# Joined changes to a five-layer kernel: order of a step in the second attention, square sums, the last projection's sides, Newton

## The chip, the core and the metric

One core of a Trainium2 chip runs the kernel. The metric is device time in microseconds of that core, median of several executions. TensorE multiplies matrices, VectorE and GpSimd do elementwise work, ScalarE activations and copies, and SP issues DMA transfers. In the profile they are PE, DVE, POOL, ACT and SP; PEld is TensorE's weight load.

## What is computed

x has 512 tokens of 1024 numbers, in float32. Four mixers come first (a conformer convolution, a forgetting attention, a short convolution, the conformer again), then one block with two attentions side by side and a feed-forward, then a last norm:

```python
def second_block(x, ...):
    h = rmsnorm(x, norm_mix)
    proj = h @ w_in                       # queries, keys, values of both attentions, gates g_br
    o_a = dsa_mixer(...)                  # 8 heads, one shared key/value, 256 best keys of 512
    o_b = nsa_mixer(...)                  # 8 heads: compressed, selected and window branch
    gate_a, gate_b = jnp.split(g_br, 2, axis=-1)
    mix = sigmoid(gate_a) * (o_a @ w_branch_a) + sigmoid(gate_b) * (o_b @ w_branch_b)
    x = x + mix @ w_out
    h = rmsnorm(x, norm_mlp)
    x = x + jnp.square(jax.nn.relu(h @ w_mlp_in)) @ w_mlp_out
    return rmsnorm(x, norm_final)
```

## The kernel before

x is kept as X, features on partitions: eight tiles of 128 features by 512 tokens. Every large product is made of float32r products of high and low parts, three for each pair of tiles (HH by WH, HL by WH, HH by WL), each 128x128 by 512 columns. The weights come in chunks of 1 MB by DMA into WR; ScalarE writes the high part (`split_hi`, WH), GpSimd the low part (`split_lo`, WL). All five engines run programs written out by hand. Semaphores order them, each `wait_ge(signal, key)` waits for the operation that carries that key, and an engine runs its program strictly in order. So what stands ahead of what in an engine's program matters.

- Start: `setup_sync` loads x (two loads), vectors, chunk 0, tap weights, two tables, chunk 1. `setup_tensor` turns x (32 transposes, L67), `setup_vector` makes each token's sum of squares (L112), and a Newton step behind a square root on ScalarE makes the factor. A diagonal matrix of the factor and `spread` bring it to all partitions. `keep_clock` issues products whose result is not used.
- Second layer A: `sum_squares(1)` adds the squares of x over features with `column_sums`, products one column wide. The last of them need the squares of tiles 6 and 7, and the factor's diagonal and its spread follow.
- Second attention: `second_tensor`'s loop of 14 steps. `PAIRS` are 12 units of two heads (eight of the second attention, two units a pair of heads, then four of the first). Step n holds, on TensorE: the turns of unit n-2's shares (`pair_turn_tensor`) in two groups of 11 and 9 transposes, the gate product of half a chunk (24 products) in two halves, each behind one group, then `pair_weigh_tensor` of unit n-2 and `pair_scores_tensor` of unit n+1. Scores of block i = 3 use banks 4 and 5, which the turns use too: the turn of (3, 1) waits until VectorE has reduced the scores (3, 0) of unit n, that of (2, 0) until it has reduced (3, 1). ScalarE evicts the turned blocks (`pair_turn_scalar`), splits a weight chunk in even steps and makes the exponentials. VectorE (`second_vector`, unchanged) goes through a step in this order: four reductions of unit n (`pair_scores_vector`, L112), four steps of the search for the best keys (up to step 6), the shares of unit n-1, four more reductions, four more steps of the search, the gate's rows, and in steps where a unit completes a bank (n = 3, 5, 7, 9 and up) a copy of the bank, which waits for the end of `pair_weigh_tensor(n-2)`. GpSimd scales shares, and from step 7 on adds mask and bias ahead of the reductions (`pair_fill_gpsimd`).
- Feed-forward: 32 products of 24, ReLU on ScalarE, square on VectorE; TensorE waits for nothing there.
- Last projection (`project_tensor(5)`): 32 tiles by 8 banks by 3 products; a bank holds 128 features of all tokens. The last two tiles are done bank by bank, so that bank n is ready six products after bank n-1. VectorE adds it to X and scales it with the last norm's gain, ScalarE squares it, GpSimd adds squares, TensorE sums them (`sum_squares(2)`) and turns the scaled tiles back to tokens on partitions (`turn_out`, 32 transposes; 16 of them stand before bank 6's products), and VectorE and ScalarE scale them into YOUT. SP stores eight half rows.

## Time and profile before

| | us |
|---|---|
| runs | 2487.3, 2487.8, 2490.5 |
| median | 2487.8 |
| profiled execution | 2488.7 |
| its span, first to last instruction | 2486.9 |
| TensorE busy | 2466.3 (99%) |
| VectorE, ScalarE, GpSimd busy | 1417.5, 1286.0, 1500.9 |
| HBM read | 302.9 MB, 124 GB/s over the span |

The granted TensorE clock is 0.998 of full in the mean. A product row in the timelines shows 0.39 us although the next one starts 0.23 us later, since they are pipelined; the cost of one is the distance of two starts. The chain of work that ended last runs through TensorE for 85% of the span and through VectorE for 9%.

### The profile page before, as it was taken

How to read it: one execution, taken by the hardware profiler on the slowest of the kernel's cores; microseconds unless marked ns; L12 is line 12 of the kernel's file. 1: busy time of each engine (PE TensorE's matmuls, PEld its weight loads, DVE VectorE, ACT ScalarE, POOL GpSimd, SP SyncE). 2: the span in 40 equal slices, each digit the busy share in tenths (PEclk: the TensorE clock that was granted, in tenths of full speed). 3: DMA queues.
4: the chain of work that ended last, by engine and by line, in shares of the span. 5: the costliest groups of instructions: out<-in, count | busy, mean ns of one | idle time of the engine just before them, and what ended most of it. 6: DMA issues, size and time to landing. Idle time of an engine off the chain costs nothing.

```text
span 2486.9 us, 31030 instructions
## 1 busy us (share of the span) xinstructions
PE 2466.3 (99%) x11629; PEld 2016.4 (81%) x11629; DVE 1417.5 (57%) x2423; ACT 1286.0 (52%) x1986; POOL 1500.9 (60%) x1017
## 2 busy tenths in 40 slices
PE   8999999999999999999999999999999999999998
PEld 6888887888888788888888888878877778888887
DVE  7999863155455524444441899986789642623102
ACT  7889744266567633222232788965345653423222
POOL 6999666453453555444455699956545556645663
PEclk9999999999999999999999999999999999999999
DMA  7888722355556323222222778862422242222221
GB/s 217 179 189 182 161 103 86 112 143 148 147 137 154 109 102 100 87 102 99 87 102 102 166 176 189 181 143 102 138 106 73 85 144 102 86 101 102 97 90 68
DMA packets 72193, 310.78 MB, mean 125 GB/s; under 512 B 8075, under 2 KB 8299, under 8 KB 58604
## 3 DMA queue, kind: packets, MB, share of 16 engines
q1 hardware_dynamic: 49164, 224.07, 26.7%
q0 software_dynamic: 22880, 84.73, 17.6%
q8 instruction: 93, 1.52, 0.2%
q14 instruction: 56, 0.46, 0.1%
HBM read 302.88 MB, written 5.89 MB: 124 GB/s over the span
## 4 chain that ended last, share of the span: by engine, by line
PE 85%; DVE 9%; POOL 2%; ACT 1%; issue 1%; DMA 1%; DVEq 0%; SPq 0%; POOLq 0%; ACTq 0%
PE ps L64 83%; DVE ps L81 6%; PE ps L67 2%; POOL AR L73 1%; POOL WL L73 1%; ACT AR L70 0%; POOL WL L115 0%; DVE ST L97 0%; DMA WL<-in_weights 0%; DVE AR L73 0%; DMA AR<-in_x 0%; DVE HL L73 0%; DVE AR L81 0%; ACT WH L70 0%; DVE AR L77 0%
## 5 line engine op out<-in xcount | busy, mean ns | idle before, releaser
L64 PE MATMUL ps<-HH,WH 128*128 128x512 f32 x3064 | 1204.4, 393 | 0.5 <-ACT WH L70 0.2
L64 PE MATMUL ps<-HL,WH 128*128 128x512 f32 x3064 | 1184.8, 389 | 0.0
L64 PE MATMUL ps<-HH,WL 128*128 128x512 f32 x3064 | 1089.8, 390 | 0.3 <-DMA WL<-in_weights 0.3
L73 POOL TENSOR_TENSOR WL<-WR,WH 128x1024 fp32r<-128x1024 f32 (+1 forms) x274 | 681.1, 2507 | 663.1 <-ACT WH L70 645.9
L64 PEld LDWEIGHTS ps<-HH,WH 128*128 128x128 f32 x3064 | 575.2, 188 | 129.8 <-ACT HH L70 4.7
L64 PEld LDWEIGHTS ps<-HH,WL 128*128 128x128 f32 x3064 | 574.7, 188 | 121.7 <-DMA WL<-in_weights 1.2
L64 PEld LDWEIGHTS ps<-HL,WH 128*128 128x128 f32 x3064 | 575.5, 188 | 118.1 <-issue 1.2
L70 ACT ACTIVATE WH<-WR 128x1024 fp32r<-128x1024 f32 (+1 forms) x403 | 408.2, 1046 | 441.6 <-PE ps L64 441.5
L81 DVE SCALAR_TENSOR_TENSOR ps<-AR,VEC,ps 128x512 f32<-128x512 f32 x652 | 448.9, 751 | 7.0 <-ACT ps L70 1.6
L73 POOL TENSOR_TENSOR AR<-AR 128x512 f32<-128x512 f32 x210 | 313.7, 1710 | 18.1 <-DVE HL L81 8.6
L70 ACT ACTIVATE AR<-ps 128x512 f32<-128x512 f32 (+3 forms) x263 | 130.6, 524 | 220.4 <-PE ps L64 140.9
L115 POOL DMA_DIRECT2D WL<-in_weights x129 | 145.2, 1125 | 132.8 <-ACT WL L70 132.8
L73 DVE TENSOR_TENSOR AR<-AR 128x512 f32<-128x512 f32 (+1 forms) x161 | 179.6, 1144 | 36.2 <-ACT AR L70 34.5
L70 ACT ACTIVATE AR<-AR,VEC 128x512 f32<-128x512 f32 x238 | 165.0, 731 | 49.3 <-DVE AR L73 31.9
L73 DVE TENSOR_TENSOR HL<-AR,HH 128x512 fp32r<-128x512 f32 x56 | 70.9, 1275 | 197.4 <-ACT HH L70 192.5
L73 DVE TENSOR_TENSOR AR<-ps,HT 128x512 f32<-128x512 f32 (+1 forms) x72 | 49.1, 687 | 221.8 <-PE ps L64 213.0
L64 PE MATMUL ps<-AR 128*128 128x128 f32 (+18 forms) x1146 | 159.6, 356 | 0.2 <-DVE AR L81 0.2
L64 PEld LDWEIGHTS ps<-AR 128*128 128x128 f32 (+5 forms) x1146 | 115.0, 174 | 42.0 <-issue 27.6
L70 ACT ACTIVATE AR<-AR 128x512 f32<-128x512 f32 (+3 forms) x72 | 40.9, 588 | 194.5 <-DVE AR L73 188.3
L73 POOL TENSOR_TENSOR AR<-AR,SQ 128x512 f32<-128x512 f32 x84 | 137.2, 1789 | 2.0
L70 ACT ACTIVATE WL<-WR 128x1024 fp32r<-128x1024 f32 x129 | 135.0, 1047 | 0.0
L73 DVE TENSOR_TENSOR AR<-AR,HT 128x512 f32<-128x512 f32 x48 | 71.3, 1485 | 97.5 <-ACT AR L70 97.0
(200 smaller groups left out, 2045.9 us busy)
## 6 DMA issues: line engine op xcount, KB each, us to landing
WR<-in_weights SPq DMA_DIRECT2D x105, 1024.0 KB, 4.8
WR<-in_weights SPq DMA_DIRECT2D x194, 512.0 KB, 4.8
WL<-in_weights POOLq DMA_DIRECT2D x129, 512.0 KB, 7.3
AR<-negc_rows POOLq DMA_DIRECT2D x16, 640.0 KB, 4.2
gate_rows<-WR SPq DMA_DIRECT2D x14, 256.0 KB, 2.9
AR<-gate_rows SPq DMA_DIRECT2D x14, 256.0 KB, 5.3
AR<-in_x SPq DMA_DIRECT2D x2, 1024.0 KB, 6.0
AR<-bias_by_distance POOLq DMA_DIRECT2D x1, 2048.0 KB, 8.6
```

Of the source, the lines that this page charges most:

```text
L64: return Op(None if self.e is None else self.e.matmul(o, l, r, start=first, stop=last, skip_group_check=True))
L67: return Op(None if self.e is None else self.e.transpose(o, i, identity))
L70: return Op(None if self.e is None else self.e.activation(o, i, f, **kw))
L73: return Op(None if self.e is None else self.e.tensor_tensor(o, a, b, op))
L81: return Op(None if self.e is None else self.e.scalar_tensor_tensor(o, a, s, b, op0, op1))
L115: return Op(None if self.e is None else self.e.dma_start(o, i, accum_op=ALU.add))
```

## The change

- x is loaded in four parts; the two small tables go behind them and behind chunk 1. TensorE runs eight 128-column products on ones before x arrives, one identity product of 512 columns ahead of the first spread, and 5 keep_clock products in place of 8 in the first layer A.
- Newton: three VectorE operations in place of four, in every rsqrt.
- `sum_squares(1)`: full-width products (128 equal columns) in place of one column.
- Second attention: step n on TensorE is first turn group, whole gate product, second turn group, scores n+1, weigh n-2. The scores of blocks (3, 0) and (3, 1) come last among the scores and wait for ScalarE's evictions of the second group. On ScalarE: evictions of the first group, weight split, four exponentials, evictions of the second group, four exponentials.
- Last projection: the activations are the stationary side, so that a bank holds 128 tokens by 512 features, and x + product is made in rows of tokens. For that, X is turned during the feed-forward (8 visits of 4 transposes after products 6 to 13) and kept as XT. The output's norm is made row by row at the end: ScalarE squares and sums a half row, VectorE makes the factor, GpSimd multiplies by the gain (loaded to all partitions), and ScalarE or VectorE scales. `turn_out`, `sum_squares(2)` and the transposes at the end are gone; the eight stores are in another order.

```diff
@@ newton @@
-            dve.tt(b, a, y, ALU.mult).then_inc(rs_dve, name, "b")
+            dve.stt(b, a, -0.5, y, ALU.mult, ALU.mult).then_inc(rs_dve, name, "b")
             dve.wait_ge(rs_dve, name, "b")
-            dve.ts(c, b, -0.5, 1.5, ALU.mult, ALU.add).then_inc(rs_dve, name, "c")
-            dve.wait_ge(rs_dve, name, "c")
-            dve.tt(r, y, c, ALU.mult).then_inc(rs_dve, name, "r")
+            dve.stt(r, b, 1.5, y, ALU.add, ALU.mult).then_inc(rs_dve, name, "r")
@@ sums of squares @@
+        def wide_column_sums(pe, o, tile, first, last):
+            for tb in range(NB):
+                op = pe.mm(o[:, tb * P:(tb + 1) * P], tile[:, tb * P:(tb + 1) * P], ones[:, :], first and tb == 0, last)
+            return op
@@ project_product @@
+            if p == 5:
+                tb, cut = slice(n // 2 * P, (n // 2 + 1) * P), slice(n % 2 * T, (n % 2 + 1) * T)
+                wh, wl = halves(WH, i)[k % 2][:, cut], halves(WL, i)[k % 2][:, cut]
+                pe.mm(b, hs(HH, s, tb), wh, k == 0, False)
+                pe.mm(b, hs(HH, s, tb), wl, False, False)
+                return pe.mm(b, hs(HL, s, tb), wh, False, k == TILES[p] - 1)
@@ project_tensor @@
-                if p == 5 and n == 5:
-                    for tb in range(NB):
-                        turn_out(pe, tb, 0, range(4))
@@ setup @@
-            for n in range(2):
-                sp.dma(t3(XIN, NB)[:, 2 * n:2 * n + 2, :], ...)
+            for tb in range(NB):
+                sp.dma(XIN[:, tb * D:(tb + 1) * D], x[0, tb * P:(tb + 1) * P, :]).then_inc(x_landed[tb], "x", by=16)
...
+            for m in range(8):
+                pe.mm(banks[7][:, 0:P], ones[:, :], ones[:, :], True, True)
...
+            pe.mm(banks[7][:, :], ident[:, :], XIN[:, 0:T], True, True)
...
-            keep_clock(pe, j, banks[1 if j else 4], 6 if j else 8)
+            keep_clock(pe, j, banks[1 if j else 4], 6 if j else 5)
@@ pair_scores_tensor @@
-            for i, e in ((3, 0), (3, 1), (1, 0), (2, 1), (2, 0), (0, 1), (0, 0), (1, 1)):
+            for i, e in ((1, 0), (2, 1), (2, 0), (0, 1), (0, 0), (1, 1), (3, 0), (3, 1)):
+                if i == 3 and u.n >= 3:
+                    pe.wait_ge(u_ev, u.n - 3, 1, e)
@@ second_tensor @@
             for n in range(14):
-                for k in range(8):
-                    for i, e in TURN_AT[k] if n >= 2 and k in TURN_AT else ():
-                        pair_turn_tensor(pe, PAIRS[n - 2], i, e)
-                    gate_part_tensor(n, (k,))
+                for i, e in TURN_GROUPS[0] if n >= 2 else ():
+                    pair_turn_tensor(pe, PAIRS[n - 2], i, e)
+                gate_part_tensor(n, range(8))
+                for i, e in TURN_GROUPS[1] if n >= 2 else ():
+                    pair_turn_tensor(pe, PAIRS[n - 2], i, e)
+                if n < 11:
+                    pair_scores_tensor(pe, PAIRS[n + 1])
                 if n >= 2:
                     pair_weigh_tensor(pe, PAIRS[n - 2])
-                if n < 11:
-                    pair_scores_tensor(pe, PAIRS[n + 1])
@@ second_scalar @@
-                if w:
-                    for i in (3, 2, 1):
-                        for e in range(2):
-                            pair_turn_scalar(act, w, i, e)
+                for i, e in TURN_GROUPS[0] if w else ():
+                    pair_turn_scalar(act, w, i, e)
                 if n % 2 == 0:
                     split_hi(act, C_GATE + n // 2 + 1)
-                if u:
-                    for i, e in BLOCKS:
-                        pair_scores_scalar(act, u, i, e)
+                for i, e in BLOCKS[:4] if u else ():
+                    pair_scores_scalar(act, u, i, e)
+                for i, e in TURN_GROUPS[1] if w else ():
+                    pair_turn_scalar(act, w, i, e)
+                for i, e in BLOCKS[4:] if u else ():
+                    pair_scores_scalar(act, u, i, e)
@@ feed_forward_tensor @@
+                if n >= 6 and n - 6 < 2 * NB:
+                    turn_x_tensor(pe, (n - 6) // 2, n % 2)
@@ the end @@
+        def square_row_scalar(act, n):
...
+            act.act(halfs(HT)[q], half_of(XT[tb], q), ACT.Square, accum_out=SUMS[:, n:n + 1]).then_inc(e_sq, n)
+        def weighted_row_vector(dve, tb, q):
...
+            dve.stt(half_of(YOUT[tb], q), half_of(XT[tb], q), small(1, "e_r", tb), half_of(GAIN, q), ALU.mult, ALU.mult).then_inc(
+                e_v, tb, q)
+        def finish_vector(dve):
...
+            add_row_vector(dve, 6)
+            factor_vector(dve, 2)
+            add_row_vector(dve, 7)
+            weighted_row_vector(dve, 2, 0)
+            factor_vector(dve, 3, 0)
+            scaled_row_vector(dve, 1, 1)
+            factor_vector(dve, 3, 1)
+            weighted_row_vector(dve, 3, 1)
```

## Rows read from the trace of the kernel before

**Rows 1.** Page, part 1: busy us, share, instructions of each engine.

```profile
PE 2466.3 (99%) x11629; PEld 2016.4 (81%) x11629; DVE 1417.5 (57%) x2423; ACT 1286.0 (52%) x1986; POOL 1500.9 (60%) x1017
```

**Rows 2.** Waits of TensorE, whole run: us in total, times, longest.

```profile
PE ps L64 <- DVE DG L73: 2.7, 4, 1.4
PE ps L67 <- DVE SM L112: 2.2, 5, 0.6
```

**Rows 3.** Timeline, TensorE: start, us, what; first pair activations as weights.

```profile
480.24 0.39 PE L64 MATMUL ps<-WH,HH 128*128 128x512 f32 x1
...
480.92 0.39 PE L64 MATMUL ps<-WH,HH 128*128 128x512 f32 x1
...
2462.05 0.39 PE L64 MATMUL ps<-HH,WH 128*128 128x512 f32 x1
...
2462.73 0.39 PE L64 MATMUL ps<-HH,WH 128*128 128x512 f32 x1
```

**Rows 4.** Chain of work that ended last, start: start, us, what.

```profile
1.28 6.99 DMA AR<-in_x
```

**Rows 5.** Windows, start: engines' busy us, TensorE's granted clock, DMA share, GB/s.

```profile
11.00:12.00 1.00, 0.58 (x6) 0.34 (x4) 0.71 (x5) 1.00 (x4) 0.00 (x0) 1.00 1.02 418
```

**Rows 6.** Timeline, ScalarE, start.

```profile
12.46 1.07 ACT L70 ACTIVATE WH<-WR 128x1024 fp32r<-128x1024 f32 x1
```

**Rows 7.** Timeline, TensorE and VectorE, head of the second layer A.

```profile
1367.97 1.34 PE L64 MATMUL ps<-ones,DG 128*128 128x1 f32 x8 [0.38 <-DVE DG L73]
1369.17 3.62 PE L64 MATMUL ps<-WH 128*128 128x512 f32 x9
1369.35 0.16 DVE L78 TENSOR_SCALAR SM<-ps 128x4 f32<-128x4 f32 x1 [1.43 <-PE ps L64]
1372.63 1.02 PE L64 MATMUL ps<-DG,ones 128*128 128x512 f32 x2
```

**Rows 8.** Windows, the same place.

```profile
1369.00:1369.50 0.50, 0.50 (x3) 0.50 (x4) 0.15 (x1) 0.00 (x0) 0.00 (x0) 0.50 0.00 0
```

**Rows 9.** Chain, first layer A: visits of four turns between products.

```profile
208.18 0.44 PE ps L67 x4
...
219.54 0.44 PE ps L67 x4
```

**Rows 10.** Timeline, second attention: VectorE's reductions and copy, TensorE's turns.

```profile
1872.41 0.67 DVE L112 CUSTOM_DVE_ANT_0 AR<-ps,AR 128x512 f32<-128x512 f32 x1
1873.15 0.66 PE L67 MATMUL ps<-ident,VEC 128*128 128x128 f32 x4 [0.30 <-DVE SM L112]
...
1897.08 0.68 DVE L84 COPY AR<-ps 128x512 f32<-128x512 f32 x1
1897.75 0.69 DVE L112 CUSTOM_DVE_ANT_0 SQ<-ps,AR 128x512 f32<-128x512 f32 x1
```

**Rows 11.** Timeline, second attention: a weigh alone and the copy behind it.

```profile
2000.33 2.38 PE L64 MATMUL ps<-AR 128*64 128x128 f32 x24
2002.76 0.69 DVE L84 COPY AR<-ps 128x512 f32<-128x512 f32 x1 [1.63 <-PE ps L64]
```

**Rows 12.** Timeline, second attention: second turn group and its evictions.

```profile
1902.95 0.49 PE L67 MATMUL ps<-ident,WR 128*128 128x128 f32 x3
1903.47 1.25 ACT L70 ACTIVATE AR<-ps 128x384 f32<-128x384 f32 x3 [2.36 <-PE ps L67]
```

**Rows 13.** Timeline, end: TensorE, VectorE, ScalarE, stores on SP.

```profile
2473.83 0.39 PE L64 MATMUL ps<-HH,WL 128*128 128x512 f32 x1
2474.25 0.69 DVE L73 TENSOR_TENSOR X<-X,ps 128x512 f32<-128x512 f32 x1 [0.17 <-PE ps L64]
2474.97 0.63 ACT L70 ACTIVATE DG<-X 128x512 f32<-128x512 f32 x1 [0.75 <-DVE X L73]
2479.70 4.47 SPq L118 DMA_DIRECT2D out_y<-AR  x8
```

**Rows 14.** Windows, second attention.

```profile
1900.00:1925.00 25.00, 25.00 (x166) 18.55 (x164) 22.44 (x68) 15.66 (x46) 14.33 (x11) 1.00 0.30 106
```

More of the change, by code:

```diff
@@ L463, in rsqrt_vector @@
         def rsqrt_vector(dve, name, src, n, scale):
-            v, s, y, a, b, c, r = (small(n, name, i) for i in range(7))
+            v, s, y, a, b, _, r = (small(n, name, i) for i in range(7))
             dve.ts(v, src, scale, EPS, ALU.mult, ALU.add).then_inc(rs_dve, name, "v")
@@ L655, in rms_vector @@
             v, r = RT[:, 4:8], RT[:, 0:4]
-            s, y, a, b, c = (small(NB, "rms", gen, i) for i in range(5))
+            s, y, a, b = (small(NB, "rms", gen, i) for i in range(4))
             dve.wait_ge(r_sum, gen)
@@ L3017, in finish_scalar @@
[L3017 to L3024 removed]
+                if n == 4:
+                    pool.wait_ge(x_new, 4, 7)
+                    pool.dma(GAIN, bass.AP(norm_final.tensor, 0, [[0, P], [1, D]])).then_inc(e_g, "landed", by=16)
@@ new lines, in build_program, with half_of, turn_x_tensor @@
+        XT = [ar(34 * T + tb * D, D) for tb in range(NB - 1)] + [SQ[:, :]]
+        YOUT = [ar(KD * T + tb * D, D) for tb in range(NB)]
+        GAIN = VEC[:, N_EARLY + 992 - D:N_EARLY + 992]
+        SUMS = small(2 * NB, "e_sums")
+        def half_of(tile, q):
+            return tile[:, q * T:(q + 1) * T]
+        def turn_x_tensor(pe, tb, q):
+            if tb:
+                pe.wait_ge(e_xt, tb - 1, q)
+            elif q:
+                pe.wait_ge(rb2_made, 5)
+            else:
+                pe.wait_ge(r_v, 5)
+            for k in range(4 * q, 4 * q + 4):
+                op = pe.turn(banks[6 + q][:, k % 4 * P:(k % 4 + 1) * P], X[:, k * T + tb * P:k * T + (tb + 1) * P],
+                             ident[:, :])
+            op.then_inc(e_t, tb, q)
@@ new lines, in root_scalar, with factor_vector @@
+        def root_scalar(act, tb):
+            act.wait_ge(e_n, tb, "v")
+            act.act(small(1, "e_s", tb), small(1, "e_v", tb), ACT.Sqrt).then_inc(e_s, tb)
+        def factor_vector(dve, tb, half=None):
+            v, s, y, b, r = (small(1, "e_" + name, tb) for name in "vsybr")
+            if half != 1:
+                dve.wait_ge(e_sq, 2 * tb + 1)
+                dve.stt(v, SUMS[:, 2 * tb:2 * tb + 1], D * EPS, SUMS[:, 2 * tb + 1:2 * tb + 2], ALU.add, ALU.add).then_inc(
+                    e_n, tb, "v")
+            if half == 0:
+                return
+            dve.wait_ge(e_s, tb)
+            dve.reciprocal(y, s).then_inc(e_n, tb, "y")
+            dve.wait_ge(e_n, tb, "y")
+            dve.stt(b, y, v, y, ALU.mult, ALU.mult).then_inc(e_n, tb, "b")
+            dve.wait_ge(e_n, tb, "b")
+            dve.stt(r, b, -3.0, y, ALU.add, ALU.mult).then_inc(e_n, tb, "r")
@@ new lines, in finish_gpsimd, with scaled_row_scalar @@
+        def finish_gpsimd(pool):
+            pool.wait_ge(e_gs, "scaled")
+            for n in (0, 1, 2, 3, 5, 6):
+                tb, q = n // 2, n % 2
+                pool.wait_ge(x_new, 5, n)
+                if n == 6:
+                    pool.wait_ge(e_n, 2, "r")
+                pool.tt(half_of(YOUT[tb], q), half_of(XT[tb], q), half_of(GAIN, q), ALU.mult).then_inc(e_zp, n)
+        def scaled_row_scalar(act, tb, q):
+            act.wait_ge(e_zp, 2 * tb + q)
+            act.wait_ge(e_n, tb, "r")
+            act.act(half_of(YOUT[tb], q), half_of(YOUT[tb], q), ACT.Copy, scale=small(1, "e_r", tb)).then_inc(e_a, tb, q)
@@ new lines, in finish_scalar @@
+        def finish_scalar(act):
+            for n in range(3):
+                square_row_scalar(act, n)
+            root_scalar(act, 0)
+            square_row_scalar(act, 3)
+            scaled_row_scalar(act, 0, 0)
+            square_row_scalar(act, 4)
+            root_scalar(act, 1)
+            scaled_row_scalar(act, 0, 1)
+            square_row_scalar(act, 5)
+            root_scalar(act, 2)
+            square_row_scalar(act, 6)
+            square_row_scalar(act, 7)
+            root_scalar(act, 3)
+            scaled_row_scalar(act, 2, 1)
+            scaled_row_scalar(act, 3, 0)
```

143 lines of the change are left out of this document (68 added, 75 removed).

## The prediction, written before the changed kernel had run

> **What bounds the kernel now.** I read the page first, then the waits of TensorE, then the timelines of the four places that the change touches. TensorE is busy for 2466.3 of 2486.9 us [rows 1], so outside the start and the end only TensorE's own work and its short waits count. The waits are few [rows 2]: 2.7 us for diagonals that VectorE makes at the head of a layer, and 2.2 us in the second attention for VectorE's score reductions (L112). Dense products start 0.68 us apart for three, 0.227 us each, whether weights or activations are the moving side [rows 3]. So turning the last projection round (p == 5) costs nothing in the stream: 768 products before and after.
>
> The sum is made against the profiled execution, 2488.7 us with a span of 2486.9; it lies 0.9 us above the median of the runs, 2487.8.
>
> **Start.** x comes in four loads, not two. The sums of squares need all of x, and the last half of it landed at 8.27 us [rows 4]. A quarter needs less, and VectorE, which had 4 x 1.2 us of sums to make from the first landing on, can begin about 1.2 us earlier and ends that much earlier; Newton gives 0.2 more: -1.35 at most. But ScalarE must split weight chunk 0 at 12.46 us between its copies of X [rows 6], and that chunk stands behind x and the vectors in a queue that still runs at its full 418 GB/s after 11 us [rows 5]; it can't be split much before 11.9. So the gain that reaches the first products lies between 0.5 and 1.35; I take **-0.8**. The warm-up products and the identity product fill TensorE's idle time ahead of the spread; keep_clock loses three products that end as HH arrives. The table loads that now wait for x on SP are needed long after; no chunk is due before them. Nothing for those.
>
> **Newton in three.** One small VectorE operation of 0.17 to 0.2 us goes in each of the rsqrt chains. TensorE waits for the diagonal in the two layer norms of layer A (part of the 2.7 us [rows 2]); there it counts, twice 0.2: **-0.4** (bounds -0.6 and 0). Elsewhere a product stream covers it.
>
> **Full-width sums before the second layer A.** Before, sixteen and eight instructions one column wide end at 1369.31; the granted clock is 0.50 of full, the 1.2 GHz level, at 1369 [rows 7, 8]. The nine keep_clock products take 3.6 us, and the spread starts at 1372.63, although the diagonal, 2.1 us behind VectorE's first operation at 1369.35, was ready at 1371.5. What TensorE did before the clock fell was three microseconds of one-column sums. Full-width ones take about the same time each (128 columns, as a turn, 0.11 us). If the clock holds at 2.4 GHz, the eight sums end at 1368.95, nine products 2.0 us later, the spread starts near 1371.0: **-1.6** (bounds -1.8; and 0 if the clock falls all the same).
>
> **Second attention.** A step n was: turns of unit n-2 (11), half of the gate product, 9 turns, the other half, weigh n-2, scores n+1. Now it is: 11 turns, the whole gate product, 9 turns, scores n+1, weigh n-2. ScalarE follows (evictions after the turns, weight split earlier). VectorE's order is not changed, and this is what I price.
> (a) Switches. A visit of four turns between products costs 11.36 - 48 x 0.2267 = 0.48 us, of which 0.44 are the turns [rows 9]. One visit less in 12 steps is 12 x 0.04 = 0.5 at least; the step also loses the change from gates to weigh; up to 12 x 0.2. I take **-1.0** (0 to -2.4).
> (b) Copy before the reductions. In steps where a bank is complete (n = 3, 5, 7, 9, 10 to 13), VectorE waits for the end of weigh n-2, copies the bank, and only then reduces scores n+1. It starts the copy 0.05 us behind weigh [rows 11], the first reduction 0.67 later [rows 10], and the turn that reuses that score bank starts 0.74 behind the reduction's start [rows 10]. Before, the scores, which stream as many columns as weigh does (2.3 us), lay between weigh and that turn and hid this. Now weigh ends the step, the first four turns (0.44) start at once and the next has to wait until 1.5 us behind weigh, the one after another 0.2: 1.2 us for each of the five steps 4, 6, 8, 10, 11: +6.0. On the other side two waits of this kind go (steps 9 and 11, where GpSimd's mask fill was late because ScalarE's weight split came late; it now comes 4 us earlier): the record shows 2.2 us in five waits [rows 2], 0.3 of them in step 2, which stays; with the pipeline's restart I count 2.7. Net **+3.3** (bounds -2.7, if VectorE's copy is somehow not in the way, and +5).
> (c) Weigh without cover. Weigh needs ScalarE's three evictions of the second turn group. They begin 0.5 us behind the first of these turns and take 1.25 [rows 12]; the turns take 0.96. Before, half a gate product (2.7 us) lay between, now 2.3 us of scores; but steps 11, 12 and 13 have no scores left: 1.8 - 1.0 = 0.8 us three times: **+2.4** (1.5 to 3).
> (d) Scores n+1 now need VectorE's reductions of n, 2.3 us earlier in the step than before. In steps 4 and 6, where VectorE starts late for (b), it is just in time by my count. Bounds 0 and two times the longest wait seen here, 0.6 [rows 2]; **+0.4**.
>
> **Turns of x in the feed-forward.** Eight visits of four turns at 0.48 [rows 9]: **+3.9** (3.5 to 4.3). ScalarE's eight copies, the gain's load and GpSimd's scaling are covered: the feed-forward has no wait of TensorE, and ScalarE and GpSimd have idle time there.
>
> **End.** Sixteen turns inside the last product group go, at 0.11 each [rows 9]: **-1.8**. Then the tail, from the start of the last product, 2473.83, to 2486.9: 13.1 us. It held the add, the square, sums on TensorE, rsqrt, turns and eight stores in one row, whose issue alone took 4.47 us from 2479.70 on; the last was issued 3.3 us before the end [rows 13]. After: add of row 7 ready 0.43 behind the last product's start, but queued behind factor 2 (which waits for ScalarE's root) until 1.3; square 0.63 [rows 13] and the read of its sum, to 2.6; v, root, three small operations to 3.8; the weighted half row (0.7) to 4.6; its store queued one issue (0.56) behind the last but one, issued at 5.3, ends 3.3 later: 8.6, with some slowing of VectorE beside GpSimd 8.8. **-4.3** (-3.3 to -5).
>
> **Sum.** -0.8 - 0.4 - 1.6 - 1.0 + 3.3 + 2.4 + 0.4 + 3.9 - 1.8 - 4.3 = +0.1. The forecast is 2488.8 in the profile's terms and **2487.9** as a median, 2485 to 2491 with its own bounds. The gains at start and end are paid back in the second attention. About 0.2% (5 us) is what a measurement of this kernel can tell from no change.
>
> **A page's rule.** In the second attention 20 turns stand in each step, and the granted clock is 1.00, the 2.4 GHz level, all the while [rows 14]. The Trainium skill (TensorE: Matmul & The Clock Gate, Part 4) says that turns don't count as activity for the clock gate in the way that products do. By that rule a stretch of turns with idle time behind it can lose the clock, which is rival 3. The rows so far show no such loss, and none is in the sum.
>
> **Rivals.**
> 1. The joining pays in full: no wait (b), (c) or (d), the old ones gone: -2.7 - 1.0 in place of +5.1 in (a) to (d): 2479.1. For it: in the steps without a copy VectorE does get its scores earlier. Against: VectorE's queue order. 0.17.
> 2. The clock falls in the one-column place as before, or the start's gain is lost: 2489.5. 0.12.
> 3. Slower: in steps 11 to 13 TensorE turns for 1 us and then waits 0.8 for ScalarE. If the granted clock falls there, as it did at 1369 [rows 8], each fall costs what that one did, where nine products took 3.6 us for 2.0 [rows 7]: 1.6, three times, +4.9: 2492.8. It decides once the clock falls in all three steps. Against: it stood at 1.00 with waits of up to 0.6 beside turns [rows 2, 14]. 0.09. The page's rule named above would have it so.
> 4. The change doesn't do what it says at the end: VectorE, not the stores, ends late, 2 us of the tail's gain go: 2489.9. 0.07.
> The forecast has 0.55.
>
> **Chances.** Faster by over 0.2% (below 2482.8): rival 1 and a little of the forecast's low end, 0.21. Slower (above 2492.8): half of rival 3 and mixtures of 2 and 4 with the bounds of (b), 0.11. Within: 0.68. The range that leaves out 2 in 10 goes from 2480 to 2492.5.
>
> **What would show it.** TensorE's waits for L112 rise from 2.2 to 5 us or more and sit at the first turn group of steps 4, 6, 8, 10 and 11; three waits for ScalarE's evictions appear ahead of the last weighs; the granted clock stays at 1.00 around 1369 and the spread follows the diagonal at once; from the last product's start to the end it is 8.8 us. If the second attention as a whole is shorter than before, (b) or (c) is wrong, and with it the forecast.

## The result: 35 us slower, and where they went

The changed kernel takes 2524.72 us (median of 4 runs, 2520.32 to 2526.91) where the kernel before takes 2489.15 (2487.3 to 2493.2) beside it: ratio 1.0138, 95% interval 1.0126 to 1.0151. The forecast was 2487.9, with a range from 2480 to 2492.5. The profiled execution took 2524.2 us, 35.5 more than that of the kernel before by their spans. Of these, 4.5 are there at VectorE's first score reduction of step 2 (1876.94 against 1872.41), 33.1 come between it and VectorE's last copy of an output (183.74 us against 150.67), and 2.1 are given back behind it.

The page of the changed kernel, its busy times (to be held against [rows 1]):

```profile
span 2522.4 us, 31016 instructions
PE 2475.9 (98%) x11620; PEld 2019.9 (80%) x11620; DVE 1441.4 (57%) x2416; ACT 1291.3 (51%) x2005; POOL 1506.8 (60%) x1021
```

TensorE has nine instructions less and 9.6 us more busy time, VectorE seven less and 23.9 us more: some instructions have become longer. The waits of TensorE over the whole run, against [rows 2] (engine, line and tile that waited, what for; us in total, times, the longest):

```profile
PE ps L64 <- DVE SM L112: 21.9, 6, 8.0
PE ps L67 <- DVE SM L112: 4.3, 6, 0.8
PE ps L64 <- ACT AR L70: 2.9, 4, 0.8
PE ps L64 <- DVE AR L73: 2.4, 1, 2.4
```

The first row is new: products (L64) that wait for VectorE's score reductions (L112), 21.9 us in six waits. The second and the third are in the main the waits of terms (b) and (c) of the prediction: five of 0.81 and three of 0.78 us; the fourth wait of the third row, 0.53, stands ahead of the scores of unit 1. The wait of the fourth row, in the index stage, was not foreseen either. TensorE's timeline shows where the first three sit (start, length, ..., in brackets the idle time before and its releaser); these are ten of its rows from 1870 on:

```profile
1874.48 2.43 PE L64 MATMUL ps<-AR 64*128 64x256 f32 x16 [1.56 <-DVE SM L112]
...
1887.88 7.13 PE L64 MATMUL ps<-AR 64*128 64x256 f32 x44 [2.55 <-DVE SM L112]
...
1908.90 0.66 PE L67 MATMUL ps<-ident,WR 128*128 128x128 f32 x4 [0.81 <-DVE SM L112]
...
1919.05 5.75 PE L64 MATMUL ps<-AR 64*128 64x256 f32 x44 [2.53 <-DVE SM L112]
...
1948.84 7.38 PE L64 MATMUL ps<-AR 64*128 64x256 f32 x44 [2.51 <-DVE SM L112]
...
1985.73 4.38 PE L64 MATMUL ps<-AR 64*128 64x256 f32 x16 [8.00 <-DVE SM L112]
...
2007.33 0.66 PE L67 MATMUL ps<-ident,WR 128*128 128x128 f32 x4 [0.81 <-DVE SM L112]
...
2019.69 6.78 PE L64 MATMUL ps<-AR 64*128 64x256 f32 x40 [4.72 <-DVE SM L112]
...
2036.27 2.38 PE L64 MATMUL ps<-AR 128*64 128x128 f32 x24 [0.78 <-ACT AR L70]
...
2058.26 2.38 PE L64 MATMUL ps<-AR 128*64 128x128 f32 x24 [0.78 <-ACT AR L70]
```

A row x44 holds the score products and the weighing behind them. It takes 5.75 us in step 4 and 7.38 in step 6, where the granted clock has fallen. It fell in steps 2, 6, 8 and 10 and stayed at 1.00 in step 4, behind a wait of 2.53 us. It falls most in steps 8 and 10; their windows (columns: busy time of TensorE, its weight loads, VectorE, ScalarE, GpSimd; then the granted clock, the DMA share and GB/s):

```profile
1980.00:1990.00 10.00, 4.27 (x16) 2.79 (x16) 6.28 (x12) 1.86 (x8) 4.48 (x5) 0.66 0.56 220
2010.00:2020.00 10.00, 5.28 (x29) 4.32 (x29) 10.00 (x15) 5.87 (x17) 9.95 (x7) 0.85 0.32 118
2020.00:2030.00 10.00, 9.19 (x56) 6.14 (x55) 3.68 (x13) 2.80 (x8) 0.77 (x2) 0.81 0.07 27
```

TensorE idles from 1977.73 to 1985.73, and the granted clock of the first window is 0.66 of full: part of it is at the 1.2 GHz level, not at 2.4. The scores and weighings behind the waits of steps 2, 6, 8 and 10 take 1.4, 1.6, 2.0 and 2.0 us more than the same products at 1.00, 7.0 in all.

All five big waits stand in even steps (2, 4, 6, 8, 10), in which GpSimd makes the low part of a weight chunk. VectorE in step 8 of the changed kernel: four of its share multiplications (L77, the scaling of a block of shares), and the first of the reductions that TensorE waits for.

```profile
1972.77 0.41 DVE L77 TENSOR_SCALAR SQ<-SQ,SM 128x384 f32<-128x384 f32 x1
1973.10 2.56 DVE L77 TENSOR_SCALAR DG<-DG,SM 128x384 f32<-128x384 f32 x1
1975.58 2.47 DVE L77 TENSOR_SCALAR HT<-HT,SM 128x256 f32<-128x256 f32 x1
1977.97 5.18 DVE L77 TENSOR_SCALAR SQ<-SQ,SM 128x128 f32<-128x128 f32 x1
...
1984.49 0.41 DVE L112 CUSTOM_DVE_ANT_0 AR<-ps,AR 128x256 f32<-128x256 f32 x1
```

And GpSimd beside it:

```profile
1972.81 5.09 POOL L73 TENSOR_TENSOR WL<-WR,WH 128x1024 fp32r<-128x1024 f32 x2 [6.99 <-ACT WH L70]
...
1978.66 1.28 POOL L73 TENSOR_TENSOR AR<-AR,MR 128x512 f32<-128x512 f32 x1
...
1981.12 3.36 POOL L73 TENSOR_TENSOR AR<-AR,MR 128x384 f32<-128x384 f32 x4
```

A share of 384 elements takes 0.41 us alone. From 1972.81, when GpSimd's subtraction begins, one takes 2.56: it stands still while one half of the subtraction (5.09 / 2 = 2.5 us) runs, gets its turn, and the next one stands still for the other half (2.47). The share of 5.18 us is another case: it starts at 1977.97, when the subtraction is over (1977.90), and lies beside GpSimd's mask fills (L73 with MR), four of which pass, behind the issue of a DMA, before it ends at 1983.16. So the subtraction is not all that VectorE meets; the fills that follow it in GpSimd's program come earlier with it. In the kernel before, the same engines in step 4 pass each other:

```profile
1903.36 1.28 DVE L77 TENSOR_SCALAR AR<-AR,SM 128x512 f32<-128x512 f32 x4
1904.55 0.42 DVE L112 CUSTOM_DVE_ANT_0 HT<-ps,AR 128x256 f32<-128x256 f32 x1
...
1905.75 4.73 POOL L73 TENSOR_TENSOR WL<-WR,WH 128x1024 fp32r<-128x1024 f32 x2 [10.24 <-ACT WH L70]
```

The shares are over 1.1 us before GpSimd begins. In the changed kernel ScalarE evicts three turns, not six, ahead of the split of the chunk, so GpSimd begins 4.2 us behind the step's first turn (1907.43 to 1911.62 in step 4) where it began 6.8 behind it (1898.95 to 1905.75), and is still at it when the shares come. The shares themselves come later, 6.7 us behind the first turn for 4.4 (1914.10 and 1903.36), most of it because VectorE starts the step late for the copy of term (b): in the kernel of experiment 2, which has the copy and not the meeting, it is 6.2, and with the copy moved (experiment 4) 4.1. Four of them then take 4.13 us instead of 1.28 in step 4, and six 8.73 in step 10. The score products of the next unit, which the change moved ahead of the weighing, wait for exactly this chain.

### The profile page after: what moved, and what is told of

It reads as the page before. It is cut to its first block, busy times and chain, and to the rows that moved or that the text cites. A ratio compares the mean times of both kernels' runs of the same rounds, so it can differ in the third digit from the quotient of the medians.

```text
span 2522.4 us, 31016 instructions
## 1 busy us (share of the span) xinstructions
PE 2475.9 (98%) x11620; PEld 2019.9 (80%) x11620; DVE 1441.4 (57%) x2416; ACT 1291.3 (51%) x2005; POOL 1506.8 (60%) x1021
## 4 chain that ended last, share of the span: by engine, by line
PE 77%; DVE 15%; POOL 3%; issue 2%; ACT 2%; DMA 1%; SPq 0%; DVEq 0%; POOLq 0%; ACTq 0%
PE ps L64 75%; DVE ps L81 10%; POOL AR L73 2%; PE ps L67 2%; DVE AR L77 1%; DMA WL<-in_weights 1%; DVE AR L73 1%; ACT AR L70 1%; POOL WL L73 1%; DVE ST L97 1%; ACT WH L70 0%; DVE SQ L73 0%; DVE AR L81 0%; DVE HL L73 0%; DMA AR<-in_x 0%
## 5 line engine op out<-in xcount | busy, mean ns | idle before, releaser
L64 PE MATMUL ps<-HH,WH 128*128 128x512 f32 x2808 | 1104.9, 394 | 3.4 <-DVE AR L73 2.4
L64 PE MATMUL ps<-HL,WH 128*128 128x512 f32 x2808 | 1085.8, 390 | 0.0
L73 POOL TENSOR_TENSOR WL<-WR,WH 128x1024 fp32r<-128x1024 f32 (+1 forms) x274 | 681.8, 2510 | 673.6 <-ACT WH L70 654.1
L64 PE MATMUL ps<-HH,WL 128*128 128x512 f32 x2808 | 990.6, 390 | 0.3 <-DMA WL<-in_weights 0.2
L64 PEld LDWEIGHTS ps<-HH,WH 128*128 128x128 f32 x2808 | 527.6, 188 | 123.7 <-issue 5.4
L64 PEld LDWEIGHTS ps<-HH,WL 128*128 128x128 f32 x2808 | 527.2, 188 | 111.7 <-DMA WL<-in_weights 1.1
L64 PEld LDWEIGHTS ps<-HL,WH 128*128 128x128 f32 x2808 | 527.8, 188 | 108.7 <-issue 1.2
L73 POOL TENSOR_TENSOR AR<-AR 128x512 f32<-128x512 f32 x210 | 313.6, 1709 | 18.1 <-DVE HL L81 8.6
L73 DVE TENSOR_TENSOR AR<-AR 128x512 f32<-128x512 f32 (+1 forms) x161 | 180.7, 1151 | 36.2 <-ACT AR L70 34.5
L64 PE MATMUL ps<-AR 128*128 128x128 f32 (+19 forms) x1146 | 166.7, 371 | 25.0 <-DVE SM L112 21.9
L73 DVE TENSOR_TENSOR HL<-AR,HH 128x512 fp32r<-128x512 f32 x56 | 71.0, 1278 | 197.2 <-ACT HH L70 192.3
L73 DVE TENSOR_TENSOR AR<-ps,HT 128x512 f32<-128x512 f32 (+1 forms) x72 | 49.1, 687 | 223.6 <-PE ps L64 214.7
L64 PEld LDWEIGHTS ps<-AR 128*128 128x128 f32 (+6 forms) x1146 | 118.6, 182 | 64.4 <-issue 26.4
L64 PE MATMUL ps<-WH,HH 128*128 128x512 f32 (+1 forms) x416 | 160.1, 385 | 0.0
L64 PE MATMUL ps<-WL,HH 128*128 128x512 f32 (+1 forms) x416 | 159.8, 384 | 0.0
L64 PE MATMUL ps<-WH,HL 128*128 128x512 f32 (+1 forms) x416 | 159.7, 384 | 0.0
```

Source lines behind the costliest of these rows:

```text
L64: return Op(None if self.e is None else self.e.matmul(o, l, r, start=first, stop=last, skip_group_check=True))
L73: return Op(None if self.e is None else self.e.tensor_tensor(o, a, b, op))
```

## Experiments

All times of a group of runs are compared with the kernel before on the same chip, 2488.7 to 2490.1 us in the four groups.

**1. Is it the order of the second attention alone?** Two kernels: the changed one with the old order of the second attention (TensorE's loop, the order inside the score products, ScalarE's loop), and the kernel before with the new order alone.

```
# old order, put back into the changed kernel: TensorE's loop (the edits of the score
# products and of ScalarE's loop are left out here)
for n in range(14):
    for k in range(8):
        for i, e in TURN_AT[k] if n >= 2 and k in TURN_AT else ():
            pair_turn_tensor(pe, PAIRS[n - 2], i, e)
        gate_part_tensor(n, (k,))
    if n >= 2:
        pair_weigh_tensor(pe, PAIRS[n - 2])
    if n < 11:
        pair_scores_tensor(pe, PAIRS[n + 1])
```

> The changed kernel with the old order of the second attention alone (turns at the two places of the gate product, score products behind the weighing, ScalarE's six evictions ahead of the split); start, wide sums, Newton and the last projection stay changed. If the whole loss lies in the joined order, the time is that of the kernel before plus 2.4 us that the index stage loses and less 2.1 us that the feed-forward and the tail give: 2489.5 us, within 2. Rival, that the other parts lose as well once they stand together: 2495 or more.

> The kernel before with the joined order of the second attention alone. If that order carries the loss by itself: 2487.8 plus the 35 us that the steps of the attention lost between the two traces, 2523 us, within 4, with the same long steps (n = 2, 4, 6, 8, 10). Rival, that the loss hangs on the 2 us by which the changed index stage moves the attention: under 2505 us.

Measured: 2485.97 us for the first (ratio 0.9986, 0.9976 to 0.9996), 2524.4 for the second (1.0130, 1.0114 to 1.0145). The order carries the loss; everything else in the change is together a gain of some 3.5 us (1 to 6 by the interval). My expectation of 2489.5, within 2, was missed by 3.5, through the index stage: the profile of the changed kernel leaves it 2.4 us later than the kernel before, this one's reaches step 2 with 2.3 us in hand (first reduction 1870.15 against 1872.41). Experiment 5 tells why. The waits of the kernel with the new order alone are those of the changed kernel:

```profile
PE ps L64 <- DVE SM L112: 22.0, 6, 8.0
```

**2. Is it the meeting of VectorE and GpSimd?** The meeting is taken away by one more wait for GpSimd, with the joined order untouched:

```
 if n % 2 == 0:
+    if 1 <= n <= 12:
+        pool.wait_ge(u_sh, n - 1, 0, 0 if n <= N_POOL_SHARES else 1)
     split_lo(pool, C_GATE + n // 2 + 1)
```

> The changed kernel with one wait more: in the even steps of the second attention GpSimd's two subtractions of the weight chunk start only behind VectorE's last share of the step. Theory (the two engines stop each other when both read and write on-chip memory alone: VectorE's shares take 4.13 us for four in step 4 where they took 1.28 before, 8.73 for six in step 10): shares go back to 1.3 to 3.1 us a step, the waits of 2.53, 2.51, 8.00 and 4.72 us in front of the score products in steps 4, 6, 8 and 10 go, and so does the fall of the clock behind them: 2494 us, within 3. Rival (the score products stand too early for VectorE anyway): waits of 2 us or more a step stay, 2510 us or more.

Measured: 2494.61 us. The five waits are gone; of the six, the one in step 1 (1.56 us), where GpSimd has no subtraction to do, stays. The three costliest waits of TensorE:

```profile
PE ps L67 <- DVE SM L112: 4.3, 6, 0.8
PE ps L64 <- ACT AR L70: 2.9, 4, 0.8
PE ps L64 <- DVE SM L112: 1.6, 1, 1.6
```

The six shares of step 10, of the 8.73 us above, have their old length again:

```profile
1984.77 1.66 DVE L77 TENSOR_SCALAR AR<-AR,SM 128x384 f32<-128x384 f32 x6
```

So 30 of the 35 us are this meeting: 20.3 us of waits, 7.0 in the products at the lower clock behind them, and the rest not traced to single rows. The wait moves the subtraction and the mask fills behind it together, so how the 30 divide between these two is not shown.

**3. The same meeting without the joined order.** In the kernel before, ScalarE's split of the chunk alone is moved ahead of the last three evictions of turns:

```
                 if w:
-                    for i in (3, 2, 1):
-                        for e in range(2):
-                            pair_turn_scalar(act, w, i, e)
+                    for i, e in TURN_GROUPS[0]:
+                        pair_turn_scalar(act, w, i, e)
                 if n % 2 == 0:
                     split_hi(act, C_GATE + n // 2 + 1)
+                if w:
+                    for i, e in TURN_GROUPS[1]:
+                        pair_turn_scalar(act, w, i, e)
```

> The kernel before, TensorE's order untouched; only on ScalarE the split of the weight chunk is moved ahead of the last three evictions of turns, so that GpSimd's subtractions begin some 3 us earlier in each even step and meet VectorE's shares. Theory of the collision: VectorE's shares of the even steps take 4 us (four) to 8 us (eight) where they took 1.3 and 3.1; steps 4 and 6 have 3.4 us of slack between the last reduction and the next score products and lose nothing or under 0.5 us each, steps 8 and 10 lose 2 to 4 us each: 2488 plus 4 to 8, so 2492 to 2496 us. Rival, that the joined order alone makes VectorE late: shares stay near 1.3 and 3.1 us and the time within 1 us of 2488.

Measured: 2491.78 us beside 2490.05; ratio 1.0007, 0.9995 to 1.0019, which can't be told from no change. The shares do meet the subtraction, and one wait arises, in step 8:

```profile
1905.29 4.15 DVE L77 TENSOR_SCALAR AR<-AR,SM 128x512 f32<-128x512 f32 x4
...
1967.02 1.57 PE L64 MATMUL ps<-AR 64*128 64x256 f32 x12 [2.05 <-DVE SM L112]
```

Step 10 loses nothing: there only the last of the eight shares was held. So my size was too large in the middle (1.7 us for 4 to 8), though the interval reaches up to 4.7. The rest holds. In step 4 of the kernel before the last reduction is over at 1905.7, and the next score products begin at about 1909.1: 3.4 us of slack, which hide four shares of 4.15 us. In the kernel of experiment 2, with the joined order, these times are 1907.9 and 1908.3: 0.4 us of slack, and in the changed kernel the same meeting makes a wait of 2.53. It takes both parts of the change together.

**4. The terms (b) and (c).** On top of the wait of experiment 2, three kernels. First, VectorE copies a finished output behind the first four reductions of the next step, not ahead of them:

```
                     for i, e in BLOCKS[:4]:
                         pair_scores_vector(dve, PAIRS[n], i, e)
+                if n >= 3 and PAIRS[n - 3].last:
+                    u = PAIRS[n - 3]
+                    dve.wait_ge(u_w, u.n)
+                    dve.copy(by_queries(u.out), by_queries(u.bank[:, :])[:, :, ::-1, :]).then_inc(u_o, u.n)
...                  # the same copy of PAIRS[n - 2] goes from the end of the step
```

> The kernel with the wait for VectorE's shares, and besides VectorE's copy of a finished output moved behind the first four reductions of the next step. Theory: the copy delayed those reductions, and with them the first product of turns, by 1.2 us at five step ends; the five waits of 0.8 us go and the time falls by 5.8 us against 2494.6, to 2488.8, within 1.5. Rival (the copy is paid in another place, the shares come later and with them turns or score products): under 2 us of it comes back.

Second, the weighing ahead of the score products again:

> The kernel with the wait for VectorE's shares, with the weighing again ahead of the score products (turns still in one visit behind the whole gate product, the copy in its old place on VectorE). Theory: the copy is then under the score products, minus 5.8 us; but the weighing stands directly behind its turns in all twelve steps, not in three, and waits 0.8 us for ScalarE's evictions in each of nine more: plus 7.2 us. 2494.6 - 5.8 + 7.2 = 2496.0 us, within 2, and twelve waits of 0.8 us for ScalarE. Rival (the weighing waits only because ScalarE has no other work in the last steps): 2489 us or less.

Third, which I call the repaired kernel, the later copy, and the second turns of steps 11 to 13 back in the middle of the gate product:

```
-                gate_part_tensor(n, range(8))
+                gate_part_tensor(n, range(4 if n >= 11 else 8))
                 for i, e in TURN_GROUPS[1] if n >= 2 else ():
                     pair_turn_tensor(pe, PAIRS[n - 2], i, e)
+                if n >= 11:
+                    gate_part_tensor(n, range(4, 8))
```

> The kernel with the wait for VectorE's shares and the later copy, and the second turns of steps 11, 12 and 13 put back into the middle of the gate product, where no score products cover them. Theory: the three waits of 0.8 us for ScalarE go, minus 2.35 us, and the joined order then has all of its gain and none of its losses: 2486.4 us, within 1.5; against the same kernel with the old order (2486.0) it is within 1 us, so joining the visits is worth nothing even without its losses. Rival, the gain that the change was after (24 switches of 0.04 to 0.1 us): 2484 us or less.

Measured: 2488.12 us (ratio 0.9994, 0.9984 to 1.0004), 2501.88 (1.0051, 1.0036 to 1.0066; 4 runs) and 2486.68 (0.9987, 0.9978 to 0.9997). Beside the 1.0017 of experiment 2, which ran on another chip, the copy cost 5.7 us by the ratios, and the uncovered weighings 1.4 by the medians, or 1.8 by the lower groups of experiment 5. The traces give it without the scatter of other stages. From VectorE's first reduction of step 2 to its last copy of an output the kernel of experiment 2 takes 156.05 us, the first of these 150.02, the third 147.55: 6.0 us for the five waits at the copy, 2.5 for the three weighings.

The second missed by 6 us. Its waits for ScalarE are as I said (12 of 0.78 and one of 0.53 make 9.9), but the turns wait in nine steps more, 0.20 us each. From its first turns to its second ones a step then takes 7.34 us where it took 6.75, and from there to the next step's 6.60 where it took 5.74. So these turn waits cost 0.6 each and the nine more weighing waits 0.86, 13.0 in all, which is what the stretch is longer (163.02 for 150.02).

```profile
PE ps L64 <- ACT AR L70: 9.9, 13, 0.8
PE ps L64 <- DVE AR L73: 2.4, 1, 2.4
PE ps L67 <- DVE SM L112: 2.0, 10, 0.2
```

The middle row is the index stage again, which leads on.

**5. The index stage.** The times of these kernels fall in two groups. The ten of the third kernel were 2483.1 to 2485.2 (five) and 2488.2 to 2489.7 us (five). The first kernel's ten fell likewise, 2485.2 to 2486.5 and 2489.7 to 2493.2. The profile of the third is of the upper group, that of the first kernel of the lower. VectorE in the index stage, the products of w1 with the position rows, first the upper one:

```profile
1759.40 1.23 DVE L73 TENSOR_TENSOR SQ<-AR 128x1024 f32<-128x1024 f32 x1 [3.73 <-issue]
1760.54 3.46 DVE L73 TENSOR_TENSOR DG<-AR 128x1024 f32<-128x1024 f32 x1
1764.03 3.30 DVE L73 TENSOR_TENSOR SQ<-SQ,DG 128x1024 f32<-128x1024 f32 x1
```

and GpSimd there:

```profile
1760.52 5.73 POOL L73 TENSOR_TENSOR WL<-WR,WH 128x1024 fp32r<-128x1024 f32 x2 [2.50 <-ACT WH L70]
```

then VectorE in the lower one, the kernel with the later copy:

```profile
1757.49 1.23 DVE L73 TENSOR_TENSOR SQ<-AR 128x1024 f32<-128x1024 f32 x1 [2.94 <-issue]
1758.63 1.22 DVE L73 TENSOR_TENSOR DG<-AR 128x1024 f32<-128x1024 f32 x1
1759.88 3.31 DVE L73 TENSOR_TENSOR SQ<-SQ,DG 128x1024 f32<-128x1024 f32 x1
```

In the upper one GpSimd began at 1760.52, 0.02 us before VectorE's second product, and VectorE lost 2.2 us. TensorE then waits 2.38 us for the key rows at 1781.65, and the group costs 5 us in all, more than the two recorded losses, which stays unexplained. In the profile of experiment 2 it was the other way round: VectorE's second product began at 1759.70, GpSimd at 1759.73, and the product took 1.22. The profile of the changed kernel is of the upper kind (3.43 us for the second product, a wait of 2.4). What releases VectorE's first product is, by the code, the load of w1; the trace names no releaser, so this is argued only. Two things race there, and the change brings this stage 2.5 us earlier; whether VectorE then loses more often is what the head of the change alone can tell. One more wait for GpSimd is tried on three kernels, and the head alone, without that wait, is a fourth:

```
+pool.wait_ge(s_pek, 0, 2)
 split_lo(pool, CS0 + 4)
```

> The repaired joined kernel with one more wait: in the index stage GpSimd's subtraction of the fourth chunk starts only behind VectorE's sum of the two products of w1. Its ten times fell in two groups, 2483.1 to 2485.2 and 2488.2 to 2489.7 us, and its profile (of the upper group) shows the second product at 3.46 us where the kernel with the later copy alone, of the lower group, has 1.22. Theory: the upper group is the executions in which GpSimd's subtraction got in ahead of that product; with the wait all executions are of the lower group: 2484.0 us median, none above 2487. Rival (the late transfer of w1 itself makes the upper group): two groups remain, median 2486 to 2487.

> The changed kernel with the old order of the second attention and the same wait in the index stage. Its lower group was 2484.1 to 2486.2, its upper 2488.8 to 2491.0 us. Theory: lower group alone, 2485.0 us median; the two orders of the attention, both without collisions, then stand within 1.5 us of each other. Rival: two groups remain, median 2486 to 2487.

> The kernel before with the wait in the index stage alone. Its fifty times lie mostly at 2487.2 to 2491.9 with eight at 2493.3 to 2495.8 us. Theory: the upper ones go; the median falls by under 1 us, ratio 0.9993 to 1.0, since VectorE's chain is seldom what TensorE waits for here. Rival: the wait makes the low parts late for TensorE, ratio 1.001.

> The kernel before with the new start, the full-width square sums and the shorter Newton step alone. By the prediction -0.8, -1.6 and -0.4: 2.8 us less, ratio 0.9989. By the traces so far (the second attention of the changed kernel with the old order begins at 1870.15 us against 1871.95 with the last projection alone): 1.8 us less, ratio 0.9993, and more executions of the upper group, as the index stage starts earlier against the transfer of w1.

Measured: 2483.76 us (11 runs, 2483.09 to 2485.13), ratio 0.9982 (0.9973 to 0.9991); 2484.40 (2483.79 to 2485.40), ratio 0.9981 (0.9972 to 0.9990); 2488.79 (2488.09 to 2490.58) and 2487.41 (2486.34 to 2492.72), both 1.0003 (0.9994 to 1.0012). With the wait the upper group is gone in the first two, which had it in five and four of ten runs. The kernel before can't tell: its median doesn't move, none of its eleven runs is high, but of the 33 without the wait beside it only two were (2494.4 and 2494.7). The head alone has an upper group in five of eleven runs (2490.9 to 2492.7), so the earlier start does make it frequent; by the medians it is 1.25 us faster than the kernel before, and my 0.9993 lies just outside the interval of its ratio. VectorE and GpSimd in the first kernel; VectorE's first product starts later here than in the upper-group profile (1760.17 for 1759.40), so a late transfer alone does not make the group:

```profile
1762.56 1.23 DVE L73 TENSOR_TENSOR SQ<-SQ,DG 128x1024 f32<-128x1024 f32 x1
...
1763.87 4.76 POOL L73 TENSOR_TENSOR WL<-WR,WH 128x1024 fp32r<-128x1024 f32 x2 [5.25 <-DVE SQ L73]
```

**6. The last projection alone,** on the kernel before.

> The kernel before with the last projection and the end alone changed (tokens on partitions, turns of x in the feed-forward, the new end); old start, sums, Newton and attention. By the sum of the prediction: turns of x +3.9, turns at the end -1.8, tail -4.3, together -2.2 us, ratio 0.9991, within 1.2 us. Rival (the tail is bound by VectorE or the last transfer and gives 2 us less): ratio 1.0000.

Measured: 2487.74 us beside 2489.19, ratio 1.0000 (0.9991 to 1.0009): by the times it stays open. Its trace tells more: from VectorE's first reduction of step 2 (1871.95) to the end (2484.5) it takes 612.55 us, the kernel before 614.49 (1872.41 to 2486.9). That is -1.94 for the -2.2 of the prediction. The head alone brings that first reduction to 1870.57, -1.84 for the -2.8, in a profile of its lower group.

**7. Does joining pay at all?** With both waits, the repaired joined order and the old one ended alike, though the joined one came to step 2 3.4 us later (first reduction 1873.61 against 1870.24 us). The score products of the first units have no turns of an older unit in front, and could keep block row 3 first, as before:

```
+three = ((3, 0), (3, 1))
+rest = ((1, 0), (2, 1), (2, 0), (0, 1), (0, 0), (1, 1))
-for i, e in ((1, 0), (2, 1), (2, 0), (0, 1), (0, 0), (1, 1), (3, 0), (3, 1)):
+for i, e in three + rest if u.n < 3 else rest + three:
```

> The repaired joined kernel with both waits, and for the first three units, which have no turns of an older unit in front of them, the score products of block row 3 first again, as in the kernel before. The repaired kernel reaches step 2 at 1873.6 us where the same kernel with the old order stands at 1870.2, and yet both end alike (spans 2483.0 and 2482.7). Theory: the joined steps give 3 us back afterwards, and the loss ahead of them is the waits of 0.53 and 1.56 us in front of the scores of units 1 and 2, which come because block row 3 stands last: without them 2483.8 - 2.1 = 2481.7 us, within 0.8, ratio to the kernel before 0.9973. Rival (the joined steps only catch up what was late, and give nothing when nothing is late): 2483.5 us or more.

Measured: 2481.88 us (8 runs, 2480.87 to 2483.0) beside 2488.89; ratio 0.9970, 0.9960 to 0.9981. This is the fastest kernel of the study, 7 us under the kernel before. From the first reduction of step 2 to VectorE's last copy of an output it takes 147.5 us (1869.50 to 2017.03), with the old order 150.7 (1870.24 to 2020.90; 1872.41 to 2023.08 in the kernel before). So the joined order, repaired, is worth 3.1 us over these steps, and 2.5 between the medians of two chips (2484.40 and 2481.88). Block row 3 first brings the rest: from the last turns of the index stage to the first ones of step 2 it takes 24.9 us in this kernel and 27.1 in that of experiment 5, so the two waits in front of the scores of units 1 and 2 cost 2.2. Of TensorE's waits for VectorE's reductions one is left:

```profile
PE ps L67 <- DVE SM L112: 0.3, 1, 0.3
```

## Why the prediction was wrong, step by step

**Term (d) failed, and it carries 30 of the 35 us.** It priced the wait of the next scores for VectorE's reductions at +0.4 us, "just in time by my count". The waits were 21.9 us in six places; five of them, with the lower clock behind them, are the 30 us of experiment 2. My count took VectorE's shares at the length they have in the old order. With that length it is right: in experiment 2, where they have it again, no wait is left in steps 2 to 10. What failed is the length, not the order of the waits. The same prediction noted under (b) that the weight split "now comes 4 us earlier", and used it only as a gain for GpSimd's mask fill. (It comes 2.6 us earlier behind the first turn of step 4.) It didn't ask what else GpSimd would meet once it begins earlier. In the tail it even allowed 0.2 us for "some slowing of VectorE beside GpSimd", and in (d) nothing. The trace of before held the price. VectorE, and GpSimd beside it, in step 7, where mask fills and shares meet in the old order too:

```profile
1941.05 5.74 DVE L77 TENSOR_SCALAR AR<-AR,SM 128x384 f32<-128x384 f32 x6
```

```profile
1941.25 1.38 POOL L73 TENSOR_TENSOR AR<-AR,MR 128x512 f32<-128x512 f32 x1
1942.58 1.40 POOL L73 TENSOR_TENSOR WR<-AR,MR 128x512 f32<-128x512 f32 x1
```

Six shares take 5.74 us here and 1.66 (at 1980.53) in step 10 of the same trace. A group of instructions whose mean hides two lengths was the sign to look for. The bound of (d), "two times the longest wait seen here", came from a trace in which the two never met at a place that counts.

The Trainium skill (SBUF — State Buffer, section "Who interferes with whom") states the rule: VectorE's tensor_scalar in its two-port mode, and its operations with two inputs in SBUF against a GpSimd operation that reads SBUF, share a port pair with GpSimd; whoever issues first holds it for the whole instruction and the other stands still. The traces agree as far as they go; the mode of an instruction they don't show. A share is held up by whole halves of the subtraction (2.56 and 2.47 us), one even by several GpSimd instructions in a row (5.18), and a two-input product by 2.2 us (3.46 for 1.22). The reductions, which read PSUM and one tile, never are: those of 256 elements take 0.41 to 0.43 us beside GpSimd and alone. An estimate from the rows of the kernel before, had I looked: two halves of 2.4 (1905.75), or 4.8 us for each even step, 24 in five, against next to no slack. The waits were 2.5 in three of the steps, where one half was met, 8.0 in step 8 and 4.7 in step 10, where both halves and the mask fills were: 20.3.

**Terms (b) and (c) were right,** in place and size. Five waits of 0.81 us stand at the first turns of steps 4, 6, 8, 10 and 11; by the traces their removal gave 6.0 us for the +6.0, by the times 5.7. Three waits of 0.78 stand ahead of the last weighings; their removal gave 2.5 us for the +2.4 by the traces, 1.4 to 1.8 by the times. The old waits, 2.7 by my count, and the switches, (a), together are worth 3.1 us by experiment 7, for 3.7; the two are not separated.

**A cost that I didn't look for.** With block row 3 last, the scores of unit 1 wait 0.53 us and those of unit 2 1.56, together 2.2 us by experiment 7. The second is a wait of the kind of (d), in step 1, which my count left out. With the index stage, and 0.6 us less than foreseen from (a) and the old waits, this is why the kernel without the meeting still lay 4.6 us above the kernel before (2494.61 and 2490.05), where my sum had +0.1.

**The clock at the head of the second layer A held** behind the wide sums, as forecast. TensorE in the changed kernel, for [rows 7]:

```profile
1364.48 2.05 PE L64 MATMUL ps<-ones,HT 128*128 128x128 f32 x16
1366.81 1.16 PE L64 MATMUL ps<-ones,DG 128*128 128x128 f32 x8 [0.27 <-DVE DG L73]
1367.72 2.31 PE L64 MATMUL ps<-WH 128*128 128x512 f32 x9
1369.99 1.12 PE L64 MATMUL ps<-DG,ones 128*128 128x512 f32 x2
```

and the window, for [rows 8]:

```profile
1364.00:1372.00 8.00, 7.73 (x43) 6.06 (x42) 3.75 (x11) 2.82 (x5) 1.28 (x1) 1.00 0.03 11
```

The granted clock is 1.00, and the spread starts at 1369.99, 2.64 us before that of [rows 7]. Of these, 1.16 were there before the sums began (1364.48 against 1365.64), for the 1.0 of start and first Newton; 1.48 come from the sums and the second Newton, for 1.8. So the start, the sums and Newton brought 2.6 of 2.8 us. The index stage then gave some of it back, and in about half of the executions of the head alone (five of eleven) all of it and more. That stage was no term of my sum: I held a gain ahead of it to pass through unchanged.

**The end was right.** From the start of the last product (2513.46) to the end (2522.4) it is 8.9 us, for the 8.8. Turns of x and the turns at the end together, +2.1 by the sum, are +2.2 (13.1 less 8.9 is 4.2, of which 1.94 remain by experiment 6).

**The rivals.** Rival 1, the joining pays in full, is not what the changed kernel did; it is what the repaired kernel of experiment 7 does, and its -3.7 was -3.1. Rival 3, the clock, had the right consequence at the wrong place: in steps 11 to 13 TensorE waits 0.78 us and the granted clock stays at 1.00 (2030 to 2060 us); in steps 2, 6, 8 and 10 it waits 2.5 to 8 us and the clock falls (in step 4, behind 2.53 us, it stays at 1.00). The rule on turns that stood beside that rival is not borne out by these three steps. No rival had VectorE's chain itself become longer. The slower rival I gave cost 4.9 us; the cause that acted cost six times that.

What stays open: whether the start, the wide sums and Newton are each worth their share. They were run together only. Open too: how the meeting divides between the subtraction and the mask fills.

## What to carry to other kernels

When a change moves an instruction of one engine earlier, go through all its neighbours in time, not only those that wait for it; VectorE and GpSimd above all, whose lengths in a trace hold only for the way they overlap there. A group with a mean far above its minimum (six shares at 5.74 and at 1.66 us) is the place to look. And a moved consumer spends slack: the same kind of meeting cost 1.7 us (at most 4.7) with 3.4 us of slack in a step, and 30 with 0.4. Check slack and lateness together; each alone looks harmless.

## What the runs showed that I had not expected

- A GpSimd subtraction of two operands (2.4 us a half) holds up VectorE's multiplications in on-chip memory, one for each half: 0.28 to 0.48 us become 2.5. It isn't always one for one: in step 8 one share of 0.28 us alone took 5.18, while GpSimd issued a DMA and made four mask fills. Reductions out of PSUM beside GpSimd keep their length (0.41 to 0.43 us for 256 elements).
- 0.02 us decided 5 us: in the index stage GpSimd in first (by 0.02 us in one profile) or VectorE in first (by 0.03 in another), after a transfer whose landing varies (VectorE idle 2.94 or 3.73 us before it). One wait more took the scatter of the repaired kernel from 6.6 us (2483.06 to 2489.68) to 2.0 (2483.09 to 2485.13).
- A recorded wait of TensorE can cost more than its length. At the turns one of 0.81 us made the step 1.20 longer and one of 0.20 us 0.6. Without a wait a group of turns starts 0.17 us before the recorded end of the one ahead (0.49 behind its start, for 0.66 of length), which the wait doesn't count; and the group behind it then starts 0.61 us later and not 0.44. Ahead of a weighing one of 0.78 cost 0.86.
